# A fused decoder kernel on one core: the first weight slabs are loaded two at a time, and the steps of the first norm come one half apart

## The reference

```
def rmsnorm(x, g):
    xf = x.astype(jnp.float32)
    y = xf * lax.rsqrt(jnp.mean(xf * xf, axis=-1, keepdims=True) + EPS)
    return (y * g.astype(jnp.float32)).astype(x.dtype)
...
        h = rmsnorm(x, mix_norm[l])
        proj = h @ w_in[l]
```

## Time and profile before

| | |
|---|---|
| median of 3 runs | 2196.88 us (2196.55 to 2197.74) |
| the profiled execution | 2194.95 us, span 2192.5 us |
| TensorE busy | 2179.9 us, 99% of the span |
| VectorE busy | 1611.0 us, 73% |
| ScalarE busy | 1315.4 us, 60% |
| chain that ended last | TensorE 96%, VectorE 2%, ScalarE 1% |
| granted TensorE clock | 0.999 on the mean |

### The profile page before, as it was taken

The page is one execution under the profiler, slowest core; times in us unless marked ns, Lnnn a source line. Parts: engine busy times, 40 slices in busy tenths (PEclk is TensorE's granted clock), DMA queues, the critical chain, the costliest instruction groups (busy, mean ns, idle before and its releaser), DMA issues.

```text
span 2192.5 us, 34406 instructions
## 1 busy us (share of the span) xinstructions
PE 2179.9 (99%) x13446; PEld 1884.0 (86%) x13446; DVE 1611.0 (73%) x2922; ACT 1315.4 (60%) x2491; POOL 9.7 (0%) x22
## 2 busy tenths in 40 slices
PE   9999999999999999999999999999999999999998
PEld 8888888888898888888888888888888888888887
DVE  7797655687687877755778867777677767698864
ACT  6866345775576666544666655555556655566754
POOL 0000000000000000000000000000000000000000
PEclk9999999999999999999999999999999999999999
DMA  7543333566455555555555555555555455544353
GB/s 269 171 142 122 116 125 130 185 224 202 164 175 192 191 187 189 191 190 186 192 188 188 191 185 190 184 183 185 191 177 172 166 195 184 190 155 146 140 208 141
DMA packets 107617, 389.29 MB, mean 178 GB/s; under 512 B 12304, under 2 KB 12560, under 8 KB 106688
## 3 DMA queue, kind: packets, MB, share of 16 engines
q1 hardware_dynamic: 105264, 377.11, 49.5%
q0 software_dynamic: 1904, 9.47, 1.2%
q10 hardware_dynamic: 288, 0.52, 0.1%
HBM read 384.34 MB, written 2.13 MB: 176 GB/s over the span
## 4 chain that ended last, share of the span: by engine, by line
PE 96%; DVE 2%; ACT 1%; issue 0%; DMA 0%; SPq 0%; DVEq 0%; ACTq 0%
PE main L498 88%; PE two L498 7%; PE two L501 1%; DVE WL L941 1%; DVE gt L941 0%; DMA RAW<-ws 0%; DVE GQ L947 0%; PE main L544 0%; ACT PP L1576 0%; ACT WH L1576 0%; DVE PP L947 0%; DVE FQ L941 0%; DVE PP L941 0%; DVE ACC L941 0%; DVE GQ L941 0%
## 5 line engine op out<-in xcount | busy, mean ns | idle before, releaser
L1576 ACT ACTIVATE WH<-RAW 128x512 fp32r<-128x512 f32 x1416 | 883.7, 629 | 679.5 <-PE main L498 674.0
L941 DVE TENSOR_TENSOR WL<-RAW,WH 128x512 fp32r<-128x512 f32 x1416 | 963.8, 689 | 401.7 <-ACT WH L1576 392.8
L498 PE MATMUL main<-A,WH 128*128 128x512 f32 (+1 forms) x3680 | 1144.9, 393 | 2.1 <-DVE WL L941 2.1
L498 PEld LDWEIGHTS main<-A,WL 128*128 128x128 f32 x3584 | 673.6, 188 | 154.9
L498 PE MATMUL main<-A,WL 128*128 128x256 f32 x3584 | 713.3, 278 | 0.0
L498 PEld LDWEIGHTS main<-A,WH 128*128 128x128 f32 x3680 | 562.6, 189 | 16.7 <-issue 10.9
L498 PE MATMUL main<-H,WH 128*128 128x512 f32 x704 | 221.1, 395 | 0.0
L498 PE MATMUL main<-B,WH 128*128 128x512 f32 (+1 forms) x640 | 184.4, 373 | 0.0
L498 PEld LDWEIGHTS main<-H,WL 128*128 128x128 f32 x704 | 132.2, 188 | 31.3
L498 PE MATMUL main<-H,WL 128*128 128x256 f32 x704 | 138.3, 278 | 0.0
L498 PE MATMUL main<-WH,A 128*128 128x512 f32 (+1 forms) x448 | 137.7, 382 | 0.0
(11 more groups left out here) (298 smaller groups left out, 1715.3 us busy)
## 6 DMA issues: line engine op xcount, KB each, us to landing
RAW<-ws SPq DMA_DIRECT2D x707, 512.0 KB, 3.2
CB<-cscr POOLq DMA_DIRECT2D x4, 1024.0 KB, 5.1
XT<-xT POOLq DMA_DIRECT2D x4, 512.0 KB, 7.6
MS<-memT POOLq DMA_DIRECT2D x4, 512.0 KB, 7.6
xs<-xT SPq DMA_DIRECT2D x7, 256.0 KB, 7.8
out<-YT SPq DMA_DIRECT2D x7, 256.0 KB, 2.6
CST<-cst SPq DMA_DIRECT2D x1, 1248.0 KB, 7.7
G<-g POOLq DMA_DIRECT2D x1, 1024.0 KB, 6.4
```

The source lines that it names most:

```text
L498: return e.matmul(o, l, r, start=start, stop=True, skip_group_check=True)
L941: return e.tensor_tensor(o, a, b, op)
L1576: return e.activation(o, i, f, bias=bias, scale=scale, accum_out=accum)
```

## The change

The loads of the first slabs are chained to landings. Pair i means x pair i and slab i. Pair 1 is issued as before. Pair 2 waits for tile 1 of x, pair 3 for slab 1, pair 4 for slab 2, and x pairs 5 to 7 for slab 3. What follows them on SyncE (slab 5 and so on) stands behind these waits. The steps of the norm's squares are moved: ScalarE issues n = 2 in step 7 and n = 3 in step 8, VectorE adds n = 1, 2 and 3 in steps 8, 9 and 10. The fold stays in step 12.

```
@@ -458,9 +458,15 @@
             e.dma_start(RAW[:, 0, 512:1024], ws[0][:, 512:1024]).then_inc(s_raw[0], 16)
             e.dma_start(xs[:, 1, :], xT[:, 1, :]).then_inc(s_x[0], 16)
             for i in range(1, NRAW):
+
+                if i == 2:
+                    w.wait_ge(s_x[0], 16)
+                elif i > 2:
+                    w.wait_ge(s_raw[i - 2], 16)
                 load_x(i)
                 load(i)
             for i in range(NRAW, 8):
+                w.wait_ge(s_raw[NRAW - 2], 16)
                 load_x(i)
             def swap(r):
 
@@ -1101,7 +1107,7 @@
             def x_sums():
                 for n in range(1, 4):
                     add_squares("x", n)
-                    yield from ticks(2)
+                    yield
 
             def x_split(kt):
                 w.wait_ge(s_Ah, kt + 1)
```

## The result

The changed kernel takes 2199.26 us (median of 20 runs, 2198.10 to 2202.15), the kernel before 2195.34 us (20 runs, 2194.89 to 2197.74). The ratio is 1.0017, 95% interval 1.0011 to 1.0023: slower by 3.9 us, 0.17%. The forecast was +0.5 us, 2197.4, with a range of 2194.9 to 2200.2. The profiled execution has a span of 2196.4 us, 3.9 above that of before.

The account below looks back on a forecast made before the run. TensorE, busy 99%, bounds the kernel; the start of the norm's matmul decides. Fold 1.24 us later, loads 0.70 us earlier: about +0.5 us, 2196.88 to 2197.4 us; range 2194.9 to 2200.2.

Parts of the forecast that it names:

- The order of the norm's steps: VectorE before the norm's matmul: two `lo`s now stand between add 3 and the fold, making it 1.24 us later.
- The circle: ScalarE and VectorE waiting for each other from 23 us (add, square, `hi`, `lo`): one turn stays 3.47 us.
- The lag: Time from a load's bytes having moved to its landing: 1.05 us taken, with 0.4 and 2.15 as ends.
- the stall of 1.07 us: TensorE's wait ending at 10.88, half 2 waiting for `lo(2)`; forecast to go as slab 1 lands earlier.
- The bytes: First loads: bytes come no sooner, x pair 5 still moved by 14.2, so ScalarE and VectorE run 0.7 us earlier.
- Rival 2: First loads: lag stays about 2 us and pacing drains the DMA engines; sum +3.2 us, 2200.1; chance 0.15.
- its own sign: Sign of the draining rival: a `hi` or split waiting for a DMA over 0.5 us between 9 and 19 us.
- The clock: TensorE's granted clock should stay 1.00, as it did through the stall of 1.83 us.
- one stall of 1.83 us: TensorE's wait ending at 33.12 in the kernel before, where the norm's matmul waits for the fold.
- 0.4 us of cover: TensorE's halves 13 to 15: new `WL` stalls cost nothing, half 15 ending at 33.9, ahead of the fold's 34.3.
- Slab 5's cover of 0.45 us: Slab 5, issued near 14.0 instead of 9.10, lands at 17.85, before ScalarE wants it at 18.3.
- What decides: Start of the norm's matmul, 33.12 us before; from there every engine's work follows at the same distances.

Follow-up runs that it names:

- e5: Norm's steps moved as in the change, loads as before, 12 unread small matmuls filling TensorE's stall before half 14; 2196.18 us.
- e12: Kernel before plus 12 unread small matmuls in front of the norm's wait for the fold; 2195.03 us.
- e10: Changed kernel plus 20 unread small matmuls, 8 before half 13 and 12 before half 14, second measurement; 2199.01 us.
- e3: Changed kernel plus 20 unread small matmuls, 8 before half 13 and 12 before half 14, first measurement; 2199.74 us.
- e11: Loads' waits alone, norm's steps as before, plus 18 unread small matmuls in front of the norm's wait for the fold; 2198.32 us.
- e1: Kernel before with the loads' waits alone, norm's steps as before; 2199.99 us, ratio 1.0019.
- e9: The changed kernel measured once more, nothing altered; 2199.93 us.
- e2: Kernel before with the moved norm's steps alone, loads as before; 2196.37 us, ratio 1.0006.
- e6: Kernel before with the waits of pairs 2 to 4 only, x pairs 5 to 7 not waiting, norm as before; 2198.54 us, ratio 1.0013.
- e7: Kernel before with one wait only, pair 2 for tile 1 of x, norm as before; 2196.72 us, ratio 1.0004.

## Why the prediction was right or wrong

**The order of the norm's steps: right.** The circle kept its turn of 3.47 us, the two `lo`s stand in front of the fold, and the fold is later by 1.09 us in the profile and the kernel by 1.15 in e5 against e12, where 1.24 were forecast. Beside the loads' waits it is 0.7 to 1.4 (e10 and e3 against e11).

**The lag: right in the profile of the change, not in all.** 1.05 us was taken, 0.8 and 1.0 were measured. Slab 1 was used at 8.72, 0.1 us behind the forecast of 8.2 to 8.6, and the stall of 1.07 us is gone. Worked out in the same way, slab 1's lag is 0.7 to 1.1 us in e1, e3 and e9, but 1.6 and 1.8 in e10 and e11, where pair 2 was issued 0.7 to 1.4 us earlier than in those. That more of pair 2's bytes then moved beside slab 1's would explain it; that is argued, not shown.

**The bytes: wrong, and this is the step that failed.** It said that "the bytes themselves come no sooner, since the engines moved data without a pause before", and that pair 5's first bytes come "just when its turn comes". No sooner was right, but they came 1.5 us later. The prediction worked out the issue of x pair 5 alone, and not those of pairs 2, 3 and 4, and left no slack between a landing and the first byte of what is issued upon it. So it let every step of the chain hide exactly behind the one before. The runs show gaps behind the landings instead: a DMA busy share of 0.49 from 7 to 8 us in the change, 0.37 and 0.45 from 9 to 10 in e10 and e11. x pair 5 was issued at 13.57 instead of the 12.7 forecast, and at 13.9 to 14.9 in e1, e3, e9, e10 and e11. Instead of 0.7 us earlier ScalarE ran 1.73 us later in the profile, and the loads cost 3.3 us in the median runs (e11 against e12).

**Rival 2** is near in size and by its own sign, a wait for a DMA of more than 0.5 us (0.73 at 13.58, 0.76 at 16.69). It held that the lag stays at 2 us, which the change's profile doesn't bear out, and that the pacing drains the engines, which is what happened, with the short lag as well. The result of +3.9 lies within the range because of that rival, whose chance of 0.15 was too low. That is in part luck: the forecast's own terms give +0.5, and the clock's share stood in no term of any sum. The text also took 0.2% as what a measurement can tell from no change; with 20 runs each the interval of the ratio is 0.06% to either side, and 0.17% is clear of it.

**The clock: wrong.** The text expected 1.00, as it did through one stall of 1.83 us in one profile. Two forecast stalls in a row are a different case, and even the single one was no safe ground: e2's profile shows the fall behind one of 1.77. It is 0.96 us of the 3.77 in the profile, and 0.97 in e9's. The prediction held that the new stalls for `WL` cost nothing, "with 0.4 us of cover"; halves 14 and 15 at half speed used that up.

**Slab 5's cover of 0.45 us: wrong.** ScalarE waited 0.74 us for it, although it ran late itself; this is the same mistake once more, since slab 5 was issued at 14.90 instead of 14.0.

**What decides: right.** The distance from the norm's matmul to the end is 2159.3 to 2159.5 us in all profiles but one, 2160.9 in e6, whose clock falls behind it.

**The base.** The absolute forecast stood on three runs of 2196.88 us; with 20 the median is 2195.34. So the difference missed by 3.4 us, the absolute time only by 1.9.

## What to carry to other kernels

A load that is made to wait for a landing should find enough queued in front of it to bridge the way from that landing to its own first byte; add up every step of such a chain, not only the last. Here, where the DMA engines had no pause before, pacing bought an earlier first slab with later ones, and the account was settled at the last loads of the burst. When two engines hand one buffer back and forth, moving the steps of the exchange in program order doesn't shorten it, and only changes which other work runs in its gaps; a second buffer does. Where a profile shows TensorE stalling for some 1.8 us or more, put the price of a clock at half speed behind it (0.96 to 1.5 us in these profiles) into the range.

## What was not expected of the hardware

The clock fell to 1.2 GHz behind a TensorE stall of 1.77 us (e2), and behind 1.44 and 1.77 us in the change and 1.43 and 1.77 in e9, though not in the profile of before with 1.83 us. The length of the last stall doesn't decide: with the same stall in front of the norm's matmul the clock fell in e6 (2.45 us) and stayed at 1.00 in e7 (2.46) and e1 (2.47). What does decide is open. The matmul in e6 and in e7:

```profile
35.25 0.86 PE L502 MATMUL two<-ACC,CST 128*128 128x256 f32 x2 [2.45 <-DVE ACC L945]
```

```profile
34.82 0.67 PE L500 MATMUL two<-ACC,CST 128*128 128x256 f32 x2 [2.46 <-DVE ACC L943]
```

In the change the clock stood at 0.50 from 34 to 37 us. In e6 it fell behind the norm's matmul, into the wide halves, and cost 1.5 us there, more than the 0.96 in the change. Its windows:

```profile
35.00:36.00 1.00, 0.75 (x3) 0.67 (x4) 1.00 (x3) 0.00 (x0) 0.00 (x0) 0.80 0.00 0
36.00:37.00 1.00, 1.00 (x5) 0.81 (x4) 1.00 (x3) 0.82 (x2) 0.83 (x2) 0.50 0.40 86
37.00:38.00 1.00, 1.00 (x4) 0.85 (x4) 1.00 (x2) 0.07 (x1) 0.16 (x1) 0.50 0.90 324
38.00:39.00 1.00, 1.00 (x5) 0.86 (x4) 0.12 (x1) 0.23 (x1) 0.00 (x0) 0.50 0.67 184
```

With everything queued, a transfer's lag behind its bytes was 1.75 and 2.15 us before; with two pairs outstanding it was 0.8 and 1.0 in the change, but up to 1.8 in e11. The Trainium skill, page "DMA: Bandwidth & Descriptors", section "Anatomy of one DMA", gives a nearly constant 2.0 us, setup and completion together, for the path through GpSimd. Here, on SyncE's path, the lag alone varies by more than a microsecond, so the whole is not constant. What makes tile 1 land anywhere from 5.8 (e10, e11) to 7.4 us (e7) is open.
